# Emptying a tile's two accumulator banks one at a time, the first one 27 gathers before the tile ends

## The reference

```python
q = (xb @ wq).reshape(PEER_BLOCK, PEER_HEADS, D_QUERY)      # and normalised
v1, i1 = lax.top_k(q1 @ k1.T, 16); v2, i2 = lax.top_k(q2 @ k2.T, 16)
sv, si = lax.top_k(v1[..., :, None] + v2[..., None, :], 16)  # 16 of 256 sums
expert = e1 * N_KEYS + e2;   g = softmax(sv)
act = gelu(einsum('phkd,pd->phk', u[expert], xb))            # a dot per expert row
out = einsum('phk,phkd->pd', g * act, v[expert])             # weighted sum of rows
x = x + g2 * out;            y = rmsnorm(x, final_norm_w)
```

## Time and profile before

| | |
|---|---|
| median of 3 runs | 3297.12 us (3294.46 to 3301.82) |
| the profiled execution: its time | 3296.16 us |
| its span | 3294.3 us |
| busy shares | PE 70%, DVE 67%, ACT 61%, POOL 37% |
| granted TensorE clock, mean | 0.677 |
| data moved | 1195.13 MB, 1113.16 MB of it by the gathers |

### The profile page before, as it was taken

One profiled execution on the slowest core, in us unless ns is written; L12 is line 12 of the kernel. 1 busy time (PEld: TensorE's weight loads), 2 busy tenths in 40 slices (PEclk: granted clock), 3 DMA queues, 4 the chain that ended last, 5 costly groups with the idle time before them and its releaser, 6 DMA issues.

```text
span 3294.3 us, 46115 instructions
## 1 busy us (share of the span) xinstructions
PE 2306.9 (70%) x15134; PEld 1144.3 (35%) x15134; DVE 2219.6 (67%) x5518; ACT 2000.6 (61%) x6402; POOL 1215.7 (37%) x1118
## 2 busy tenths in 40 slices
PE   7999987988668666666666666666666666666544
PEld 5665464333234333333333233223333332232110
DVE  5687256877667767666766676667666766676645
ACT  3332055777666666666666666666666666666655
POOL 0000102344434444444444444444434444443433
PEclk9999997899656556555655565556556655565555
DMA  7232327999999999999999999999999999999998
GB/s 285 87 104 76 81 72 289 390 392 395 405 385 420 420 420 405 420 420 420 395 420 421 419 399 420 420 420 394 420 420 420 395 420 420 420 397 419 421 421 344
DMA packets 184164, 1195.13 MB, mean 363 GB/s; under 512 B 22122, under 2 KB 32906, under 8 KB 44530
## 3 DMA queue, kind: packets, MB, share of 16 engines
q0 software_dynamic: 154240, 1113.16, 82.5%
q1 hardware_dynamic: 29684, 79.02, 6.8%
HBM read 1182.83 MB, written 9.25 MB: 362 GB/s over the span
## 4 chain that ended last, share of the span: by engine, by line
DMA 49%; PE 24%; ACT 10%; DVE 8%; issue 5%; POOL 3%; SPq 1%; DVEq 0%; POOLq 0%; ACTq 0%
DMA r_w<-in_peer_uv,gidx 21%; DMA r_qk<-in_peer_uv,gidx 12%; DMA r_yT<-in_peer_uv,gidx 11%; PE ps L777 6%; PE ps L1030 5%; PE ps L834 3%; PE ps L966 3%; DMA r_vo<-in_peer_uv,gidx 3%; PE ps L926 2%; PE ps L1017 2%; DVE r_w L1971 2%; ACT mixc L1375 2%; POOL r_vo L681 2%; ACT mixc L1374 1%; DVE r_qk L1971 1%
## 5 line engine op out<-in xcount | busy, mean ns | idle before, releaser
L1371 ACT ACTIVATE mixc<-mixc 128x1 f32<-128x1 f32 x1056 | 212.4, 201 | 797.6 <-DVE r_qk L1971 212.0
L681 POOL DMA_INDIRECT r_vo<-in_peer_uv,gidx x273 | 337.9, 1238 | 647.4 <-PE ps L1030 591.1
L1030 PE MATMUL ps<-r_qk 128*32 128x256 f32 x2192 | 273.1, 587 | 374.9 <-ACT r_qk L1379 334.2
L681 POOL DMA_INDIRECT r_qk<-in_peer_uv,gidx x274 | 284.3, 1038 | 413.7 <-PE ps L1030 371.8
L1375 ACT ACTIVATE mixc<-mixc 128x1 f32<-128x1 f32 x1056 | 409.2, 388 | 35.2
L1030 PE MATMUL ps<-r_w,r_qk 128*32 128x256 f32 x1880 | 245.2, 614 | 250.1 <-ACT r_qk L1379 236.8
L681 POOL DMA_INDIRECT r_yT<-in_peer_uv,gidx x274 | 314.6, 1148 | 255.1 <-PE ps L1030 200.6
L1374 ACT ACTIVATE mixc<-mixc 128x1 f32<-128x1 f32 x1056 | 395.1, 374 | 1.0
L1379 ACT ACTIVATE r_qk<-prm,mixc 128x32 f32<-128x32 f32 x1056 | 340.3, 322 | 34.3
L681 POOL DMA_INDIRECT r_w<-in_peer_uv,gidx x235 | 245.4, 1044 | 276.3 <-PE ps L1030 258.2
L1030 PE MATMUL ps<-r_yT,r_qk 128*32 128x256 f32 x2192 | 230.7, 530 | 131.0 <-ACT r_qk L1379 116.4
(11 more groups left out here) (331 smaller groups left out, 4297.1 us busy)
## 6 DMA issues: line engine op xcount, KB each, us to landing
r_w<-in_ada_w SPq DMA_DIRECT2D x18, 1024.0 KB, 5.4
r_w<-in_w_lin SPq DMA_DIRECT2D x16, 512.0 KB, 8.1
r_w<-in_peer_wq SPq DMA_DIRECT2D x6, 1024.0 KB, 24.2
r_hT<-in_peer_wq SPq DMA_DIRECT2D x6, 1024.0 KB, 21.8
r_yT<-in_peer_uv,gidx POOLq DMA_INDIRECT x274
r_qk<-in_peer_uv,gidx POOLq DMA_INDIRECT x274
r_vo<-in_peer_uv,gidx POOLq DMA_INDIRECT x273
r_vo<-in_x_prompt SPq DMA_DIRECT2D x8, 512.0 KB, 7.0
```

Of the source, the lines that this page charges most:

```text
L681: pool.indirect_dma_start(ring[i], None, table, bass.IndirectOffsetOnAxis(gidx_t[:, t % 2, h, c:c + 1], 0)).then_inc(e_ld[i], 16)
L1030: mm = nc.tensor.matmul(ps[c * DEC:(c + 1) * DEC, q // 2, (q % 2) * QC:(q % 2 + 1) * QC], diag[:, s % 4, :], row[:, D + c * QC:D + (c + 1) ...
L1371: wch.mark(nc.scalar.activation(sq[:, i:i + 1], d, ACT.Square, scale=GELU_C ** 0.5 / TANH_K))
```

## The change

The tile's finish is cut in two, one half for each bank, each with its own signal `acc_free[0]` and `acc_free[1]`. For tiles 1 to 7 the first half (bank 0) is multiplied and added after the tile's own dot 101, and its two sums of squares follow after dot 103. For tile 0 both come after dot 1 of tile 1. The second half (bank 1) comes after dot 3 of the next tile as before, its squares after dot 5. PE's wait moves from the first mix of a tile to the first mix into each bank: for bank 0 that is still the tile's first slot, for bank 1 it is slot 32 (slot 16 in tile 1). PE's sum of the squares comes after mix 8 instead of mix 6. A half also waits for `x_rep`, since it overwrites token rows that PE copies from.

```diff
-                if t and s == t * TILE_SLOTS:
-                    pe.wait_ge(acc_free, t)
+                if t and s == spans[t, q // 2][0]:
+                    pe.wait_ge(acc_free[q // 2], t)
...
-                if t and j == 6:
+                if t and j == 8:
                     sum_squares(t - 1, 4)
...
+            def final_half(t, i, nq):
+                if i == 0:
+                    fc.base, fc.n = t * K_FIN, 0
                 n = min(nq, 2)
+                a = h2h(t, i)[:, 0:n * QC].rearrange("p (q n) -> p q n", q=n)
+                dve.wait_ge(v_free, RING + spans[t, i][-1] + 1)
+                dve.wait_ge(x_rep, 2 * replicated[t])
                 dve.wait_ge(g2_ld, 192)
+                V.tensor_tensor(a, ps[:, i, 0:n * QC].rearrange("p (q n) -> p q n", q=n),
+                                (g2b if nq == 4 else g2s).unsqueeze(1).broadcast_to([P, n, QC]), ALU.mult).then_inc(acc_free[i], 1)
+                dve.wait_ge(acc_free[i], t + 1)
                 dve.wait_ge(x1_ld, t * 64 + 64)
+                fc.mark(V.tensor_tensor(a, a, x1s[:, 2 * i:2 * i + n], ALU.add))
...
+                if 0 < t < NT - 1 and j == 101:
+                    final_half(t, 0, 4)
+                if 0 < t < NT - 1 and j == 103:
+                    final_squares(t, 0, 4)
+                if t == 1 and j == 1:
+                    final_half(0, 0, 4)
+                    final_squares(0, 0, 4)
                 if t and j == 3:
-                    final_sum(t - 1, 4)
+                    final_half(t - 1, 1, 4)
-                if t and j == 4:
-                    final_square(t - 1, 4)
+                if t and j == 5:
+                    final_squares(t - 1, 1, 4)
```

More of the change, by code:

```diff
@@ L46 @@
 NEG_MAX = -3.0e38
-K_ROUTE, K_W, K_FIN = 14, 3, 5
+K_ROUTE, K_W, K_FIN = 14, 3, 6
 QUADS, NG = 4, 16
@@ L284, in build @@
         e_ld = [sem(f"e_ld{j}") for j in range(PLACES)]
-        dot_done, dg_ready, v_free, acc_free = (sem(n) for n in ("dot_done", "dg_ready", "v_free", "acc_free"))
+        dot_done, dg_ready, v_free = (sem(n) for n in ("dot_done", "dg_ready", "v_free"))
+        acc_free = [sem(f"acc_free{i}") for i in range(2)]
         s_tr, s_ev = sem("s_tr"), sem("s_ev")
@@ L379, in build @@
         first.append(N_SLOTS)
+        replicated = [sum(x[0] <= t for x in builds) for t in range(NT)]
         spans = {}
@@ L1975, in y_quads, with final_squares @@
                 return [h2h(t, q // 2)[:, q % 2 * QC:(q % 2 + 1) * QC] for q in range(nq)]
-            def final_sum(t, nq):
-                fc.base, fc.n = t * K_FIN, 0
+            def final_half(t, i, nq):
+                if i == 0:
+                    fc.base, fc.n = t * K_FIN, 0
                 n = min(nq, 2)
-                parts = [h2h(t, i)[:, 0:n * QC].rearrange("p (q n) -> p q n", q=n) for i in range((nq + 1) // 2)]
-                dve.wait_ge(v_free, RING + (t * TILE_SLOTS + TILE_SLOTS if nq == 4 else N_SLOTS))
+                a = h2h(t, i)[:, 0:n * QC].rearrange("p (q n) -> p q n", q=n)
+                dve.wait_ge(v_free, RING + spans[t, i][-1] + 1)
+                dve.wait_ge(x_rep, 2 * replicated[t])
                 dve.wait_ge(g2_ld, 192)
[L1983 to L1987, removed]
+                V.tensor_tensor(a, ps[:, i, 0:n * QC].rearrange("p (q n) -> p q n", q=n),
+                                (g2b if nq == 4 else g2s).unsqueeze(1).broadcast_to([P, n, QC]), ALU.mult).then_inc(acc_free[i], 1)
+                dve.wait_ge(acc_free[i], t + 1)
                 dve.wait_ge(x1_ld, t * 64 + 64)
[L1989 to L1993, removed]
+                fc.mark(V.tensor_tensor(a, a, x1s[:, 2 * i:2 * i + n], ALU.add))
+            def final_squares(t, i, nq):
                 fc.need()
-                for q, a in enumerate(y_quads(t, nq)):
+                for q in range(2 * i, min(2 * i + 2, nq)):
+                    a = y_quads(t, nq)[q]
                     last = V.scalar_tensor_tensor(fdump, a, 1.0, a, ALU.mult, ALU.mult, accum_out=fss[:, q:q + 1])
@@ L1998, in final_square @@
                         fc.link(last)
-                last.then_inc(f_sq, 1)
+                    else:
+                        last.then_inc(f_sq, 1)
             def final_variance(t, nq):
@@ L2007, in final_scale @@
                 fc.link(V.reciprocal(frs[:, 0:nq], frs[:, 0:nq]))
-                assert fc.n == nq + 1
+                assert fc.n == (K_FIN if nq == 4 else 2)
                 for q, a in enumerate(y_quads(t, nq)):
@@ L2134, in _ @@
                         copy_places(m)
-            final_sum(NT - 1, 1)
-            final_square(NT - 1, 1)
+            final_half(NT - 1, 0, 1)
+            final_squares(NT - 1, 0, 1)
             final_variance(NT - 1, 1)
```

## The result

The changed kernel takes 3303.62 us (median of 12 runs, 3299.37 to 3308.03) beside 3296.97 us for the kernel before (12 runs, 3292.29 to 3301.82): a ratio of 1.0018, 95% interval 1.0011 to 1.0026. That is 6.7 us, a loss of a fifth of a percent, small but real, since the interval lies above 1. The forecast was 3301 us. The profiled execution took 3306.39 us.

A forecast was written before the change was run, and what follows sets the result against it. The stream of 1056 gathers on DMA (49% of the chain) was taken as the bound. 3296.16 - 0.3 (boundaries) + 5 (tile 1) = 3300.9, with 0.96 for the median 3301.8; predicted 3301 us, range 3284 to 3308.

The forecast's parts named there:

- The dips at boundaries 2 to 8 cost 0.3 us: Starts of tiles 2 to 8: removing PE's wait for the multiply gains 0.3 us by window lengths, bounds 0 and 17.9.
- The rival that counted the mean rate (3284): Boundaries 2 to 8: the dip in mean GB/s counts in full, 17.9 us gained, 3284 us; chance 0.14.
- The early half at dots 101 and 103: DVE, late in each tile: 2.2 us of finish work fits in its free time between dots; cost taken as 0.
- the sums after mix 8: PE's sums of squares now behind its query in most tiles: cost 0, at most 1 us of DVE's free time.
- Tile 0's early half costs 5 us: Start of tile 1: DVE's wait for the late residual now stands ahead of dots 2 and 3; 5 us lost, bounds 0 and 9.0.
- Gathers 8 and 9 go out earlier and bridge the gap: Start of tile 1: mix 0 no longer waits until 920.08, so two earlier gathers keep the DMA fed for 5 us.
- the rival at full price: Start of tile 1: gather 10 is 9.0 us late and all of it reaches the stream, 3306 us; chance 0.15.
- The absolute times at tile 1: Start of tile 1: DVE's residual wait lasts 11 us or more, and dot 14 starts near 953 in place of 948.25.

The follow-up runs named there:

- only tile 0 early: Changed kernel's finish for tile 0 only; tiles 1 to 7 finished as in the kernel before: 3303.16 us, ratio 1.0018 to the kernel before.
- before, loads first: Kernel before, with SP's loads of tile 0's residual, gate and norm's weights moved ahead of 4 MB of query weights: 3294.03 us, ratio 0.9990.
- the five kernels with the halves: Changed kernel (3303.62 us) and four variants keeping its split finish in tiles 1 to 7, with tile 0's finish or load order altered: 3298.45, 3299.20, 3292.77, 3294.84 us.
- the three that finish tiles 1 to 7 as before: Kernel before (3297.17 us), it with residual and gate loads ahead of query weights (3294.03), and the changed kernel's finish for tile 0 only (3303.16).
- the two longer stalls: Kernel before, with the finish of tiles 1 to 7 one dot later (3306.36 us) or three dots later (3340.14 us).
- The three with the loads first: Residual, gate and norm's weights loaded ahead of query weights: in the changed kernel 3292.77 us, the one before 3294.03, the changed one with tile 0's old finish 3294.84.
- finish three dots later: Kernel before, with the finish of tiles 1 to 7 after dot 6, squares after dot 7, sums after mix 8: 3340.14 us, ratio 1.0124.

## Why the prediction was right

The forecast was no change with a small loss: 3301 us for a measured 3303.62. The loss was 4.7 us by its sum (5 - 0.3) and came out as 6.7.

*The dips at boundaries 2 to 8 cost 0.3 us.* Right in that it is next to nothing; the size was read from one trace. Ten gathers take nearly as long without the dip (175.91 and 176.91 us for seven windows), but the two other traces with these dips have 179.99 (only tile 0 early) and 177.65 us (before, loads first), so a window of ten gathers doesn't settle a tenth of a us. By the table, the five kernels with the halves need 2344.59 us behind dot 14 on the mean, and the three that finish tiles 1 to 7 as before, at the old place, 2345.73. That is 1.1 us where 0.3 stood, and the three alone lie 2.8 us apart; the medians (3298.45 against 3297.17, 3294.84 against 3294.03) show no gain at all. The rival that counted the mean rate (3284) falls, by these and by the two longer stalls. A rule of the Trainium skill (Perfetto Trace Analysis, section Identifying the Most-Contended Engine) judges DMA by its throughput, and then asks which DMA resource actually binds. The trace shows why the second half is needed: throughput rose in the windows and time didn't fall, for what binds is the last part of a gather. That the parts ahead fall back in the stall while the last ones keep their pace is shown by the landings; that the same DMA engines bring the last parts in every tile was argued and not shown, since no count tells its engine.

*The early half at dots 101 and 103, and the sums after mix 8, cost nothing.* Right within what can be measured: with tile 0 as before and all the rest of the change, the ratio is 1.0001 (3 us to either side), and the slots around dot 101 take as long as before (352.62 and 352.94 us).

*Tile 0's early half costs 5 us.* Right within its bounds of 0 and 9, and somewhat low. With the other tiles alike, it costs 5.2 us (3303.62 - 3298.45) and 6.0 us (3303.16 - 3297.17) by medians, each known to some 3 us. In traces with an equal landing of the residual it is 6.8 us at dot 14 (952.37 to 959.20), where 4.5 to 5.3 stood. The step that was too small is PE's: gather 10 was to go out 6.4 us behind the residual's add (934.3 - 927.86), and it went out 9.1 us behind it (936.12 - 926.98, 940.33 - 931.18). A copy of token rows, 2.07 us on PE (L1019), stands ahead of mix 2 and waited there too; I had counted DVE's steps and the mix. In the rows it waits for a row copy on ACT (936.31), which is queued behind the weight of dot 2, and dot 2 (933.71) is only 0.3 us later behind the add than worked out. So 2.4 of the 2.7 us arise between dot 2 and its mix, where these copies stand. No run moves the copies.

*Gathers 8 and 9 go out earlier and bridge the gap.* Half right. The multiply has a wait of its own, for the gate, which before was over by the time DVE came to it (no wait at 918.65 in the earlier trace rows). Where the gate came at 914.41, gather 8 went out at 917.13; in the changed kernel's trace it came at 918.70, and gather 8 (921.41) was 0.55 us earlier than before (921.96). Still the rival at full price falls: with only tile 0 early gather 10 was 10.8 us later than before (936.12 - 925.33), and the loss is 6. With a missed wait and a missed copy in the sum, that the total came within 3 us of the measured one is in part luck.

*The absolute times at tile 1.* Dot 14 at 959.20 in place of 953 is the landing of the residual, 3.3 us later in this execution than in the one before (931.18, 927.86), and 2.7 us more from the add to dot 14 than worked out (28.02 against 953.2 - 927.86 = 25.3). Gather 10 is 2.7 us later behind the add as well, but with only tile 0 early, where it is just as late, dot 14 is 26.97 us behind the add; so the lateness of gather 10 is not all of it, and what else there is stays open.

## What to carry to other kernels

A dip in mean DMA throughput is worth what the latest part of a transfer loses by it: measure how long the transfers take to land, over the dip and over the whole tile behind it, before you price it, and know that a stall is free only up to a margin, here 1.2 to 1.8 us more than the kernel had. When work is moved ahead, look at every wait it takes along and ask when its data land in the place where it would now stand; a load that was late but hidden turns into a stall for all that is queued behind the waiter. The cure for such a wait is the order of the loads on their queue: it was worth 3 us on the kernel before and 11 on the changed one, by the medians.

## What the runs showed that I had not expected

The times scatter more with the old order of the loads. The kernel before ran from 3290.44 to 3304.16 us over 60 runs, and the five others that load in its order and finish at most one dot later spread by 8 to 14 us each. The three with the loads first spread by 4.6 to 5.8 us, over 11 runs each. In the traces that load in the old order the add begins anywhere from 926.98 to 933.00. That this landing makes the scatter is likely and not shown: the four runs that finish three dots later load in the old order too and spread by 3.4 us.
